# Last tiles taken out one stage later, rows stored by heads, and other layouts of the state-space scan, in a two-block fp32 mixer model

## What is computed

```
first_block:
  for i in (0, 1):
    h = rmsnorm(x, norm[i]); p = h @ w_in[i]           # to attention inputs and a gate
    y = concat(attention 1(p), attention 2(p))         # 16 heads of 128
    x = x + (y * silu(gate)) @ w_out[i]
  x = rmsnorm(x, norm_f)
second_block:
  p = rms_norm(x, norm_w) @ w_in                       # all branches' inputs and the gates
  o_a = gdn_branch(...)      # gated delta rule: rms_norm(o, norm_w) * silu(z), 8 heads
  o_b = rwkv7_branch(...)    # group norm, bonus, silu(z), 16 heads
  o_c = s5_branch(...)       # 64 groups, 64 complex states each:
        x_t = a * x_{t-1} + B u_t;  y_t = Re(C x_t) + d u_t;  then gelu and a gated linear unit
  merged = sum over branches of sigmoid(gates + gate_b) * (branch @ w_branch)
  out = rms_norm(x + merged @ w_out)
```

## Time and profile before

| | us |
|---|---|
| median of 3 executions | 2782.49 |
| the profiled execution's own time | 2787.1 |
| its span in the trace | 2785.3 |
| PE busy | 2439.2 |
| DVE busy | 1617.1 |
| ACT busy | 1080.9 |
| POOL busy | 96.2 |
| mean granted PE clock, share of full | 0.944 |

### The profile page before, as it was taken

How to read it: one execution, slowest core, us unless ns; L and a number is a source line. 1 busy time by engine, 2 the same in 40 slices (tenths; PEclk the granted TensorE clock), 3 DMA queues, 4 the chain that set the end, 5 groups by cost and what they waited for, 6 DMA issues and landing times. The chain is left out here.

```text
span 2785.3 us, 31171 instructions
## 1 busy us (share of the span) xinstructions
PE 2439.2 (88%) x12188; PEld 2014.2 (72%) x12188; DVE 1617.1 (58%) x2295; ACT 1080.9 (39%) x1470; POOL 96.2 (3%) x161
## 2 busy tenths in 40 slices
PE   6989577899999587998999989897999899879997
PEld 5777355788888477776878777785678788767875
DVE  4588666554443254546877585545954544546764
ACT  4433144444443554452232463223543222225443
POOL 0100000100000001000000100001010000010100
PEclk9999799999999899998999999998999999989998
DMA  6667531865566236666554643238684232257763
GB/s 212 203 221 250 200 104 42 307 207 204 204 221 221 103 98 220 229 206 234 167 174 136 216 136 114 91 93 298 217 292 136 78 116 87 73 197 242 254 188 117
DMA packets 225938, 494.82 MB, mean 178 GB/s; under 512 B 16064, under 2 KB 34592, under 8 KB 220672
## 3 DMA queue, kind: packets, MB, share of 16 engines
q1 hardware_dynamic: 206592, 398.54, 42.6%
q0 software_dynamic: 19200, 94.28, 9.3%
HBM read 429.27 MB, written 63.51 MB: 177 GB/s over the span
## 5 line engine op out<-in xcount | busy, mean ns | idle before, releaser
L156 DVE TENSOR_TENSOR mm_lo<-mm_raw,mm_hi 128x1024 fp32r<-128x1024 f32 (+4 forms) x664 | 791.4, 1198 | 580.0 <-ACT mm_hi L149 572.7
L149 ACT CAST mm_hi<-mm_raw 128x1024 fp32r<-128x1024 f32 (+4 forms) x664 | 680.5, 1028 | 1000.9 <-PE mm_acc L238 928.7
L238 PE MATMUL mm_acc<-mm_hi,mm_aT_hi 128*128 128x512 f32 (+4 forms) x2176 | 892.5, 410 | 140.6 <-DVE mm_lo L156 91.7
L238 PE MATMUL mm_acc<-mm_lo,mm_aT_hi 128*128 128x512 f32 (+4 forms) x2176 | 861.1, 396 | 0.0
L238 PE MATMUL mm_acc<-mm_hi,mm_aT_lo 128*128 128x512 f32 (+4 forms) x2176 | 860.1, 395 | 0.0
L238 PEld LDWEIGHTS mm_acc<-mm_hi,mm_aT_hi 128*128 128x128 f32 x2176 | 427.3, 196 | 247.3 <-issue 68.4
L238 PEld LDWEIGHTS mm_acc<-mm_hi,mm_aT_lo 128*128 128x128 f32 x2176 | 425.2, 195 | 85.4
L238 PEld LDWEIGHTS mm_acc<-mm_lo,mm_aT_hi 128*128 128x128 f32 x2176 | 427.7, 197 | 74.6 <-issue 1.0
L200 ACT ACTIVATE mm_stage<-mm_acc,mm_row_scale 128x512 f32<-128x512 f32 (+4 forms) x128 | 79.5, 674 | 103.0 <-PE mm_acc L238 103.0
L238 PE MATMUL mm_acc<-mm_hi,in_yT_hi 128*128 128x512 f32 x256 | 102.8, 402 | 3.6 <-DVE mm_lo L156 3.6
L238 PE MATMUL mm_acc<-mm_lo,in_yT_hi 128*128 128x512 f32 x256 | 101.9, 398 | 0.0
(11 more groups left out here) (581 smaller groups left out, 2469.8 us busy)
## 6 DMA issues: line engine op xcount, KB each, us to landing
mm_raw<-in_w_in SPq DMA_DIRECT2D x456, 512.0 KB, 5.2
mm_raw<-in_w_out SPq DMA_DIRECT2D x96, 512.0 KB, 5.2
proj<-mm_stage SPq DMA_DIRECT2D x57, 512.0 KB, 3.1
mm_raw<-in_w_branch SPq DMA_DIRECT2D x48, 512.0 KB, 5.3
mm_raw<-in_w_in SPq DMA_DIRECT2D x32, 416.0 KB, 4.7
home_tab<-s5t_tab POOLq DMA_DIRECT2D x4, 2048.0 KB, 7.7
s_tab<-home_tab POOLq DMA_DIRECT2D x8, 1024.0 KB, 5.6
odd_pr<-proj SPq DMA_DIRECT2D x2, 3076.0 KB, 14.8
```

The source lines that it names most:

```text
L149: self.nc.scalar.copy(self.hi[:, c % RING, :, 0:t.w], self.raw[:, c % RAW, :, 0:t.w]).then_inc(self.hi_done, 1)
L156: self.nc.vector.tensor_tensor(self.lo[:, c % RING, :, 0:t.w], self.raw[:, c % RAW, :, 0:t.w], self.hi[:, c % RING, :, 0:t.w].bitcast(F32) ...
L238: last = nc.tensor.matmul(self.acc[s][m][:, 0:t.w], t.aT[a][:, k, m * P:(m + 1) * P], b[:, c % RING, k - k0, 0:t.w], start=(k == 0 and fir ...
```

## The change

**Last tiles.** `seam` and every mixer call `sp_out` and `act_out` at their start, not at their end; the last tile of a stage is taken out of PSUM in the next stage, and the barrier doesn't wait for its store. Loads that need it wait for the store inside the next stage.

**Attention.** `even`: ticks 7, 6, 3, 4 and 4 behind the last unit (was 7, 6, 4, 7, 0). `odd`: 3, 10, 7 and 4 (was 3, 12, 9, 0). `y` is stored by POOL in four pieces, each when its heads are done.

**gdn, rwk.** The norm of gdn's first quad lies in the second quad's chain; the output is stored by quad by POOL (gdn 2, rwk 4 pieces). `carry` stays in SBUF. In rwk the norm's weights `lnw` are loaded into `tT["al"]` when a quad's `y` is done, X and nS lie in `tT["be"]`, and POOL loads the tail's `yt` and identity (`TailRows`).

**State space.** ACT takes the two tiles of `u` straight into SBUF (`t.dest`), with no store and load; identity, B, C, `mag` and `dd` are loaded by POOL in the seam `in2` (`S5Rows`). In a step DVE subtracts and adds the four terms to two (`state`), and PE has half the matmuls behind it. Points are 72 for 72 ticks.

```diff
@@ Stream.act_out
-                if t.stores > 1:
+                if t.dest is None and t.stores > 1:
                     act.wait_ge(self.stored[s], 16 * (t.stores - 1))
+                dest = self.stage[:, s, :, 0:t.w] if t.dest is None else t.dest
                 for m in range(MT):
-                    last = self.nc.scalar.activation(self.stage[:, s, m, 0:t.w], ...
+                    last = self.nc.scalar.activation(dest[:, m, :], ...
@@ seam, block.sync
+                mm.sp_out(sp)
                 sp.dma_start(ident[:, :], C["ident"]).then_inc(const_in, 16)
...
-                mm.sp_out(sp)
-                mm.wait_stored(sp, list(first) + list(projected))
+                mm.wait_stored(sp, first)
@@ even_mix
-        n_rope, n_dots, n_top = n_all * 5 // 16, n_all // 4, n_all * 3 // 16
+        n_rope, n_dots, n_top, n_end = n_all * 5 // 16, n_all // 4, n_all // 8, n_all // 6
...
+                mm.sp_out(sp)
                 mm.wait_stored(sp, needed)
                 for m in range(MT):
                     sp.dma_start(pr[:, m, :], prv[:, m, 0:EVEN_MIX]).then_inc(x_in, 16)
...
+            @block.gpsimd
+            def _(pool):
+                pool.wait_ge(soft.o_done, MT * N_B)
+                pool.dma_start(yv[:, :, N_A * HD:D], pr[:, :, C_QB:C_QB + N_B * HD]).then_inc(stored, 16)
+                done = MT * N_B
+                for m, h0, h1 in ((0, 0, N_A), (1, 0, N_A // 2), (1, N_A // 2, N_A)):
+                    done += h1 - h0
+                    pool.wait_ge(soft.o_done, done)
+                    pool.dma_start(yv[:, m, h0 * HD:h1 * HD], pr[:, m, h0 * HD:h1 * HD]).then_inc(stored, 16)
+                pool.wait_ge(stored, 64)
...
                 soft.tensor(pe, soft_pace)
+                mm.pe(pe, n_end)
@@ odd_mix
-        n_turn, n_c = n_all // 8, n_all // 2
+        n_turn, n_c, n_end = n_all // 8, n_all * 5 // 12, n_all // 6
@@ gdn, block.vector
+                        if q and m == 0:
+                            mean_square(q - 1)
+                    if q:
+                        normed(q - 1)
                     inv.vector(dve, q, [M[:, m, :] for m in range(MT)], pace)
@@ rwkv, block.gpsimd
+                early(pool)
                 for q in range(NQ):
-                    if q:
-                        pool.wait_ge(s["normed"], q)
...
+                    pool.wait_ge(s["y_done"], MT * (q + 1))
+                    for i, w in enumerate((lnx_w, lnx_b)):
+                        pool.dma_start(lnw(q)[:, i, :], bcast_rows(w[c])).then_inc(s["lnw_in"], 16)
+                    pool.wait_ge(s["normed"], q + 1)
+                    pool.dma_start(out.rearrange("(m p) n -> p m n", p=P)[:, :, c], y[:, :, c]).then_inc(s["stored"], 16)
@@ s5_scan, block.vector
-                    if j >= 2:
-                        dve.wait_ge(s["y_step"], j - 1)
                     dve.wait_ge(s["step"], both)
-                    TT(q1[:, j % 2, :, :], o, ro, ALU.mult).then_inc(s["q_done"], 1)
-                    TT(q2[:, j % 2, :, :], swap(o), ro, ALU.mult).then_inc(s["q_done"], 1)
+                own = step(TT(q1[:, :, :], o, ro, ALU.mult))
+                other = step(TT(q2[:, :, :], swap(o), ro, ALU.mult))
+                if j >= 2:
+                    dve.wait_ge(s["y_step"], j - 1)
+                dve.wait_ge(s["step"], own)
+                TT(state[:, j % 2, 0, :], q1[:, 0, :], q1[:, 1, :], ALU.subtract).then_inc(s["q_done"], 1)
+                dve.wait_ge(s["step"], other)
+                TT(state[:, j % 2, 1, :], q2[:, 0, :], q2[:, 1, :], ALU.add).then_inc(s["q_done"], 1)
                 pace.dve(dve)
@@ tail
-                sp.dma_start(ident[:, :], C["ident"]).then_inc(y_in, 16)
-                sp.dma_start(yt[:, :, :], rowsv(yg)).then_inc(y_in, 16)
+                mm.sp_out(sp)
...
-                pool.wait_ge(y_in, 32)
                 pool.dma_start(ab[:, :, :], rowsv(oa)).then_inc(a_in, 16)
```

More of the change, by code:

```diff
@@ L469, in ticks, with seam @@
     return sum(t.KT // KC for t in tiles)
-def seam(nc, name, C, mm, x, projected, behind, mixed=None, norms=(), rows_out=None, clear=None):
+def seam(nc, name, C, mm, x, projected, behind, mixed=None, norms=(), rows_out=None, clear=None, early=None):
     NB, NN = D // TN, len(norms)
@@ L1903, in _, with rwkv @@
                 pace.dve(dve, 2)
-def rwkv(nc, name, C, mm, needed, behind, proj, al, be, ka, rh, vv, bonus, carry, lnx_w, lnx_b, out):
+def rwkv(nc, name, C, mm, needed, behind, proj, al, be, ka, rh, vv, bonus, carry, lnx_w, lnx_b, out, early):
     W, CH = R_W, MT
@@ L2026, in _ @@
                 for q in range(NQ):
+                    X, nS = (tT["be"][:, 2 * q + i, :] for i in range(2))
                     def products(b, lhs, rhss, m):
@@ L2562, in tail, with __init__, load @@
-def tail(nc, name, C, mm, glu, branch, last, proj, yg, oa, ob, glu_b, gate_b, x, norm, out):
+class S5Rows:
+    def __init__(self, ph, tiles, tables, d, C):
+        self.ph, self.tiles, self.tables, self.d, self.C = ph, tiles, tables, d, C
+        self.mag = ph.sb("mag", [P, NJ])
+        self.BT = ph.sb("BT", [P, 2, JJ, P])
+        self.CT = ph.sb("CT", [P, 3, JJ, P])
+        self.ident = ph.sb("ident", [P, P])
+        self.u = ph.sb("u", [P, MT, S_W])
+        self.dd = ph.sb("dd", [P, S_W])
+        self.const_in, self.skip_in = ph.sem("const_in"), ph.sem("skip_in")
+        for t in tiles:
+            t.dest = self.u[:, :, t.c0 - O_SU:t.c0 - O_SU + t.w]
+    def load(self, pool):
+        home_mag, home_BT, home_CT, home_tab = self.tables
+        flat = lambda t: t[:, :, :, :].rearrange("p a b c -> p (a b c)")
+        pool.dma_start(self.ident[:, :], self.C["ident"]).then_inc(self.const_in, 16)
+        pool.dma_start(flat(self.BT), home_BT).then_inc(self.const_in, 16)
+        pool.dma_start(flat(self.CT), home_CT).then_inc(self.const_in, 16)
+        pool.dma_start(self.mag[:, :], home_mag).then_inc(self.skip_in, 16)
+        pool.dma_start(self.dd[:, :], bcast_rows(self.d)).then_inc(self.skip_in, 16)
@@ new lines, with __init__, load, tail @@
+class TailRows:
+    def __init__(self, ph, yg, C):
+        self.ph, self.yg, self.C = ph, yg, C
+        self.yt = ph.sb("yt", [P, MT, S_W])
+        self.ident = ph.sb("ident", [P, P])
+        self.y_in = ph.sem("y_in")
+    def load(self, pool):
+        pool.dma_start(self.ident[:, :], self.C["ident"]).then_inc(self.y_in, 16)
+        pool.dma_start(self.yt[:, :, :], self.yg.rearrange("(m p) d -> p m d", p=P)).then_inc(self.y_in, 16)
+def tail(nc, name, mm, early, glu, branch, last, proj, oa, ob, glu_b, gate_b, x, norm, out):
```

459 lines of the change are left out of this document (232 added, 227 removed).

## The result

| | before | changed |
|---|---|---|
| median of 4 executions, us | 2782.44 | 2712.06 |
| range | 2780.45 to 2784.75 | 2709.69 to 2713.57 |
| profiled execution: its time, its span | 2787.1, 2785.3 | 2711.58, 2709.7 |
| mean granted PE clock | 0.944 | 0.950 |

The ratio is 0.9741 (95% interval 0.9725 to 0.9757): 2.6% faster. 2717 were forecast, 5 too many; the range was 2701 to 2741.

What follows compares the result with a forecast made beforehand. PE bounds the kernel (busy 88%), with long waits nearly all at stage boundaries. Gains 44 + 10 + 5.5 + 3.7 - 0.8 + 1 + 2 + 2 = 67.4, less 2 for extra loads, gave 2717 us, range 2701 to 2741.

Steps and rivals of the forecast that it cites:

- the early loads: Seam and rwk: extra loads moved ahead were expected to cost time; 2 us taken off the summed gain.
- The step of the scan: Scan: PE sets the step, halved output products save 0.85 us a step, 8.57 to 7.72; 27.2 us over 32 steps.
- The scan's start: Before the scan's first tick and turning: waits of 5.20 and 12.40 go, 15.6 us gained, plus 2.4 for the clock.
- rwk to tail: Boundary of 13.21 us: only ob's last quarter still goes out and yt is already there; gain 10 us, between 7 and 11.
- The ends of the attention layers: Ends of even and odd: four ticks behind the last unit cover the store; gains 5.5 us in even, 3.7 in odd.
- The exchange at the starts: Before even and odd: shorter boundary against later input load, -4.5 us at even's start; these boundaries together -0.8.
- (b): Rival: starts of even, odd, gdn and rwk lengthen, or ticks were cheaper; 14 us less gained, 2731; chance 0.14.
- gdn, rwp and rwk: gdn: norm in the chain loses 5 us, shorter end wins 7, so 2; rwp and rwk: 2 (-3 to 6).
- (d): Rival: the scan's step becomes a round trip between DVE and PE, 9.9 us a step; 2787 from 9.8 on; chance 0.03.
- (a): Rival: DVE binds the scan, a step of 8.2 us gives 15 us back; 2732; chance 0.15.
- (e): Rival: more is won, stage starts fully covered and both falls of the clock gone; 2700; chance 0.07.

Runs made afterwards that it cites:

- e1: Changed kernel with the four terms of the scan's state again multiplied by PE, without DVE's two small instructions; 2742.08 us, ratio 0.9845 to the kernel before.
- e11: Kernel before with only the scan's step changed: DVE makes two terms of four, PE has half the output products; 2755.62 us, ratio 0.9896.
- e5: Changed kernel with identity, B, C, mag and dd loaded by POOL at the scan's start, not in the seam in front; 2726.71 us, ratio 0.9792.
- e7: Changed kernel with the tail's rows yt and identity loaded by SP at the tail's start; 2725.03 us, ratio 0.979.
- e3: Changed kernel with both attention layers' ticks as before, none behind the last unit, y still stored in pieces by POOL; 2710.2 us, ratio 0.9728.
- e4: Changed kernel with the last tile again taken out and stored before both attention layers, at the end of the preceding stage; 2707.75 us, ratio 0.9726.
- e6: Changed kernel with the norms of both gdn quads at gdn's end, stores still by quad; 2716.97 us, ratio 0.9758.
- e2: Changed kernel with two more DVE instructions of 128x256 in each scan step, whose results nobody reads; 2722.7 us, ratio 0.9774.
- e8: Changed kernel without ticks behind the last unit, attention inputs in two pieces, low parts and ticks moved to starts, identity and gdn's small loads first; 2708.05 us.
- e12: Changed kernel with attention ticks as before, last tile taken out before even, odd's inputs in two pieces behind the last tile's store; 2703.59 us, ratio 0.9708.
- e10: Changed kernel with yt and identity loaded at the tail's start, POOL holding its other loads until yt has landed; 2718.87 us, ratio 0.9761.

## Why the prediction held, step by step

The time came out within 5 us of the forecast, and part of that is luck: terms that were missed on both sides made up for one another. Between the two traces, which differ by 75.6, the scan with its start and the gap behind it won 52.8 where 45 were forecast (the upper bound for the scan and its start was 48), and gdn 6.3 where 2 were. The attention layers and the boundaries around them (in0, even, odd, the gap in front of odd) won 3.5 where 8.4 were. Rwp and rwk won 1.0 of 2, the way from rwk to the tail 8.8 of 10, and the rest of the seams 3.0, where 2 were taken off for the early loads. And the traces overstate the gain by 5.2 against the medians.

**The step of the scan.** Forecast 7.72 with DVE at 7.37, measured 7.67 with DVE at 7.41; 27.2 forecast, 28.5 and 29 measured by e1 and e11. The mechanism held: PE sets the step. 8 records took 0.90 less, 0.11 each. The Trainium skill (TensorE: Matmul & The Clock Gate, Back-to-back issue gap) has a floor of about 25 ns between starts of matmuls this small; the 0.11 lies far above it, so that it was right to go by the row. The Trainium skill (VectorE: DVE Perf Modes, The TRN2 errata) gives 0.42 for such a DVE instruction; the trace agrees for the time that is listed (0.42), not for the distance of starts (0.33 and 0.34).

**The scan's start.** From the marks, the scan gained 48.9, of which the step has 28.5, and the gap in front of it, 3.9, counts to in2. So the start and the gap behind won 24.3 (48.9 - 28.5 + 3.9), against 15.6 + 2.4 + 1 forecast. The idle time in it fell by 16.0 (5.20 and 12.40 became 1.29 and 0.33) and the gap behind by 1.7, near the 15.6 and 1 forecast. Most of the rest is clock. In the kernel before, the matmuls of the first tick stood 0.43 apart at the lower level and the tick took 5.20, in the changed kernel 2.81, so 2.4; the turning and the tick behind the wait took 7.5, now 4.8 without their own wait, so 2.6 more: it fell twice, where one was counted and the second named as perhaps. The last 1.6 is a single step of 10.14 in the trace of before, at a granted clock of 0.83 and with PE busy all the time. e11 has no such step, so that this is not the change's. Behind the scan the changed kernel's clock stays at 1.00 for 10 us of gdn, and falls only after a wait of 4.42 for gdn's convolution weights (0.79 from 1525 to 1531); what that won counts to gdn. The 2 taken off for early loads were wrong: e5 shows no cost in the seam.

**rwk to tail.** Forecast 10, measured 8.8 (13.21 to 4.42). The parts named for the 13.21, landings of 5.0 and 5.0 and a barrier of 1.1, add up to 11.1 only. The gap is 4.4 where I had 3: the last quarter of ob is issued at 2410.0, so the chain is 2.6 of landing and a barrier behind a late norm. What I had wrong was the price of what went away: e7 shows that the load would have cost 14 without POOL's wait.

**The ends of the attention layers.** This is the step that failed. The fall of the boundary from 11.99 to near 5 was credited to the four ticks behind the last unit, whose cost at full length was to be the price of it. The boundary became 5.45, but 6.36 without any tick (e3), so that the ticks bought 0.9 there and 1.5 behind odd, and cost about 3.5 net in even and 1.4 in odd. In even a tick in the softmax loop gives back less than I took: between the first and the last unit, three fewer ticks gave 5.8 from e3's trace to the changed one (59.3 to 53.5), and 6.5 or 2.2 each on the average of all traces, not 2.8, which is more than the whole tick of 2.73. In odd four fewer gave 7.2, where 6.9 were forecast. What the ends won in all is read from e4, where the starts wait as in the kernel before: even is 197.0 against 199.2 and 200.8 (e11), so 2.2 to 3.8 instead of 5.5; odd 176.2 against 181.5 and 180.4, so 4.3 to 5.3 instead of 3.7.

**The exchange at the starts.** -4.5 forecast in front of even, -3.9 measured; in front of odd it is an even exchange, as forecast. Both came from reading the boundary and the next load as one chain. That means that rival (b), starts that lengthen, was half true; it was in the sum already.

**gdn, rwp and rwk.** 2 forecast for gdn, 6.3 measured, of which e6 puts 5.2 down to the norm's place. The term mis-sized was "5 lost" in the chain: the wait there grew by 2.7 (3.43 to 6.16). A part of the 6.3 can be the clock at gdn's start, which was 0.86 in the first 21 us before and is 0.94; the gdn of before takes 324.0 in e11, where it was 0.92. For rwp and rwk 2 were forecast and 1.0 came; the gap behind rwp is 3.03, not 1 to 2, and 3.0 to 7.3 in the other traces, so that this term can't be judged.

Some sums of the forecast don't come out, none by enough to matter: even's -1.3 + 7.0 is 5.7 and odd's -2.1 + 6 is 3.9, where 5.5 and 3.7 were taken; the boundaries' 4.2 - 4.5 is -0.3, not -0.8; and in (d) a step of 9.8 costs 39, not 43.

The other rivals: (a), DVE binds, did not happen, though e2 shows it about 0.3 us away; (d), a round trip, has nothing in its favour, as PE's rows in the step stand without a gap; of (e), more is won, the two falls of the clock at the scan's start did go away.

## What to carry to other kernels

Before work is kept back to cover a store at a stage's end, cut the store so that its last piece is small, and read how long that takes: here 3 us against 11 us of ticks. Before a stage's gain of a few us is put down to a change, look at the same stage in traces that left it alone: here even alone varies by 3.4 us. A tile's take-out that moves into the next stage wins only where nothing at the next start waits for it, and where the barrier had waited for it. When a load is moved ahead, look for the wait that held other transfers back for its sake; one goes with the other.

## What was not expected of the hardware

A store of 416 KB took 20.7 us to land when it was issued behind 6 MB of loads on the same queue (e8), and 3.3 when it was issued ahead of them (e12). One MB took 13.9 us beside POOL's loads and 5.9 with these held back (e7, e10). And 3.1 MB of loads beside a full stream of weights (165.5 us for the seam in either case, e5) cost nothing that the trace shows.

The granted clock isn't the same in every execution of the same code: in0 ran at 0.997 in the trace of before and at 0.964 in e11's, with PE busy for 74.3 and 77.1 us. That is why in0 won only 2.1 us between the two traces although the gap behind it fell by 4.2 (5.23 to 1.02). What lowered the clock there stays open.
